# Softmax attention in another order on TensorE, four buffers of turned weights, and changed layer ends

## The chip, the cores and the metric

The kernel runs on one core of a Trainium2 chip. The metric is the device time of one execution in microseconds (us); a smaller number is better. An execution is profiled once, and its time, its span (first to last instruction) and its rows come from that one execution.

## What is computed

The reference runs a transformer of four layers over 512 tokens of width 1024, in float32. The first two layers also carry 256 context tokens. They have a gated linear attention, a neighbourhood attention and a sliding-window attention; the last two have an attention over selected keys and an mLSTM. Each layer ends in a gated feed-forward network (FFN). The part that the change reorders is the softmax of these attentions, cut here to what it comes to:

```python
s_loc = einsum('bnqhgd,bnkhd->bhgnqk', qb, kb) * scale      # local keys, masked with -inf
s_ctx = einsum('bnqhgd,blhd->bhgnql', qb, kc) * scale       # context keys
p = softmax(concatenate([s_loc, s_ctx, s_sink], axis=-1))   # s_sink only in the sliding window
o = einsum('bhgnqk,bnkhd->bnqhgd', p_loc, vb) + einsum('bhgnql,blhd->bnqhgd', p_ctx, vc)
```

## The kernel before, in words

The program is written by hand for each engine: the order of the code is the order in which an engine runs it, and semaphores tie the engines together. There is no scheduler. A layer is: norm and modulation of the activations, the input projection (`product`, L611), the token mixers, the output projection, the FFN (`gate_up` L1082, then `product` again), and a layer end. Products are in float32 made of three matmuls of rounded parts: each operand is split into a high part (L1319 for weights, L1327 for activations, on ACT) and a low part (L1823 and L1835 on DVE).

**The softmax loop.** `softmax_attention` works through units; a unit is one head by one tile of 128 queries against n keys. Two units make a pair p. Layer 0 has 36 pairs: 6 of 256 keys, 12 of 512, 6 of 256, and then 12 of the sliding window (3 of 512, 6 of 640, 3 of 512). Layer 1 has the 24 of these that are not of 256 keys. Layers 2 and 3 have 16 each: 4 of 128, 4 of 256, 4 of 384 and 4 of 512 keys, in that order. For one unit:

- PE computes the scores, queries by keys (`scores`, L825 and L826, both units of a pair together).
- DVE adds the bias or mask, negates, and takes the row extreme (`weigh`, L1908) into one of four score buffers SB.
- ACT takes the exponential in place and the row sum (`exp`, L1489).
- PE transposes the weights in blocks of 128 by 128 (`turned`, L838) into bank PS[4] for the even unit, PS[5] for the odd.
- The turned weights are copied to a buffer PB: the even unit by DVE (L1947), the odd by ACT (L1504). There are two such buffers, one for each.
- PE multiplies the turned weights with the values (`values`, L851) into bank PS[7].
- After each group of units DVE divides by the row sum (`output`, L1924 to L1933), which frees PS[7].

PE's order in a pair is: turn both units, scores of pair p+1, values of both units. DVE's order is: copy of the even unit, weigh the two units of pair p+1. ACT's is: copy of the odd unit, then two exponentials of pair p+1.

**The start of a layer's projection.** `turn_normed` and `turn_norm` transpose the normed activations, one f for each 128 of their 1024 columns (L644 for f = 0 and 1, L632 for the others; six tiles each). ACT and DVE split each into high and low parts. In layer 1 the first chunk of the product goes through f (there called k) in turn, four tiles and 12 matmuls of 428 columns for each; it waits for the low part (`normed_low0`). The transposes of f = 4 to 7 (`turn_beside`) stand between the parts of the product.

**The layer end.** After the last product PE runs `warm(8)` (L571), 16 matmuls on constants whose result nobody reads. In the meantime DVE adds the gated result to the residual and ACT sums its squares (L1447). In layer 1 the mean and root go through eight small ACT operations (L1457, L1458) and four square roots (L1462). In layers 2 and 3 GpSimd (POOL) multiplies the FFN's output with a gain (L1291) while DVE adds it tile by tile to the residual (L2437). DVE's last reciprocal (L2576) ends the layer. Then all engines meet at a barrier (L2659), behind which the next layer's first operations start (L1356 on ACT, L1805 on DVE). There is no barrier inside a layer.

## Time and profile before

| | |
|---|---|
| time, median of 3 runs | 3622.78 us (3615.99 to 3623.82) |
| time of the profiled execution | 3606.66 us |
| its span | 3604.9 us |
| its mean granted TensorE clock | 0.959 of full speed |
| PE busy | 3352.9 us (93% of the span) |
| PEld (weight loads) busy | 2721.4 us (75%) |
| DVE busy | 2003.1 us (56%) |
| ACT busy | 1122.1 us (31%) |
| POOL busy | 194.1 us (5%) |
| 16 DMA engines | 92 GB/s of reads and writes of HBM over the span |

Busy is the time in which an engine runs an instruction; PEld is the loading of a matmul's stationary operand, which overlaps the matmul before. The granted clock is the share of TensorE's full clock that the chip gave it: 1.00 is 2.4 GHz and 0.50 is 1.2 GHz, and an average between them is a mixture in time. A share of the whole span says little about one stage; the stages are read by window.

### The profile page before, as it was taken

To read this page: it belongs to the slowest core of one execution; us is meant where nothing else is said; L and a number is where in the kernel's file an instruction comes from. 1 tells how busy PE (TensorE), PEld (TensorE's weight loads), DVE (VectorE), ACT (ScalarE), POOL (GpSimd) and SP (SyncE) were. 2 spreads that over 40 slices of the span, in tenths; PEclk is the share of its full clock that TensorE was granted. 3 is DMA by queue.
4 is the path that set the end of the run, shared out by engine and by line. 5 is a ranking of instruction groups with operands and counts; after the bars stand their busy time and mean duration, and the time that the engine had idled before them with its cause. 6 is when DMAs were issued, how large, how long until landed. Compare 5 with 4: busy or idle time off the path is not lost. (4 is left out here: it accounts for less than half of the span.)

```text
span 3604.9 us, 44421 instructions
## 1 busy us (share of the span) xinstructions
PE 3352.9 (93%) x17758; PEld 2721.4 (75%) x17758; DVE 2003.1 (56%) x3595; ACT 1122.1 (31%) x1926; POOL 194.1 (5%) x187
## 2 busy tenths in 40 slices
PE   6998999999999997999999998799999998699998
PEld 4986777888888895777877775467877775468886
DVE  4666655846564425557555556667445555653334
ACT  3113454111112412442222433542222433542222
POOL 0000000000000000000000143000000242000001
PEclk9998999999999997999999997799999997899999
DMA  5441102533231211117444230026443230023332
GB/s 207 131 133 39 51 19 74 152 98 113 94 114 58 68 45 42 52 55 227 151 140 135 74 94 30 1 75 212 154 150 115 88 87 18 0 65 100 92 101 76
DMA packets 316574, 336.23 MB, mean 93 GB/s; under 512 B 11944, under 2 KB 219344, under 8 KB 316368
## 3 DMA queue, kind: packets, MB, share of 16 engines
q1 hardware_dynamic: 316368, 333.39, 29.7%
q8 instruction: 141, 2.31, 0.3%
q14 instruction: 65, 0.53, 0.1%
HBM read 329.67 MB, written 3.67 MB: 92 GB/s over the span
## 5 line engine op out<-in xcount | busy, mean ns | idle before, releaser
L1823 DVE TENSOR_TENSOR weights_low<-weights,weights_high 128x1024 fp32r<-128x1024 f32 (+5 forms) x416 | 488.0, 1175 | 850.2 <-ACT weights_high L1319 848.6
L1319 ACT ACTIVATE weights_high<-weights 128x1024 fp32r<-128x1024 f32 (+5 forms) x416 | 419.8, 1011 | 1311.9 <-PE banks L611 874.8
L1082 PE MATMUL banks<-h_high,weights_high 128*128 128x512 f32 (+1 forms) x1760 | 655.5, 372 | 20.7 <-DVE h_low L1835 12.8
L1082 PE MATMUL banks<-h_low,weights_high 128*128 128x512 f32 (+1 forms) x1760 | 648.8, 369 | 0.0
L1082 PE MATMUL banks<-h_high,weights_low 128*128 128x512 f32 (+1 forms) x1760 | 648.4, 368 | 0.0
L611 PE MATMUL banks<-weights_high,h_high 128*128 128x512 f32 (+4 forms) x1360 | 509.3, 374 | 11.4 <-DVE h_low L1835 6.7
L611 PE MATMUL banks<-weights_high,h_low 128*128 128x512 f32 (+4 forms) x1360 | 500.6, 368 | 0.0
L611 PE MATMUL banks<-weights_low,h_high 128*128 128x512 f32 (+4 forms) x1360 | 499.0, 367 | 0.0
L1082 PEld LDWEIGHTS banks<-h_high,weights_high 128*128 128x128 f32 x1760 | 332.1, 189 | 87.8 <-DVE h_low L1835 14.4
L1082 PEld LDWEIGHTS banks<-h_high,weights_low 128*128 128x128 f32 x1760 | 332.0, 189 | 56.0
L1082 PEld LDWEIGHTS banks<-h_low,weights_high 128*128 128x128 f32 x1760 | 332.4, 189 | 52.7
L611 PE MATMUL banks<-weights_high,hidden_high 128*128 128x512 f32 x792 | 311.1, 393 | 15.3 <-DVE weights_low L1823 15.3
L611 PE MATMUL banks<-weights_high,hidden_low 128*128 128x512 f32 x792 | 309.0, 390 | 0.0
L611 PE MATMUL banks<-weights_low,hidden_high 128*128 128x512 f32 x792 | 308.9, 390 | 0.0
L611 PEld LDWEIGHTS banks<-weights_high,h_high 128*128 128x128 f32 x1360 | 257.3, 189 | 54.2 <-issue 21.4
L611 PEld LDWEIGHTS banks<-weights_high,h_low 128*128 128x128 f32 x1360 | 257.1, 189 | 28.5
L611 PEld LDWEIGHTS banks<-weights_low,h_high 128*128 128x128 f32 x1360 | 257.6, 189 | 27.3 <-issue 1.0
L2545 DVE TENSOR_TENSOR projected<-projected,banks 128x512 f32<-128x512 f32 (+1 forms) x110 | 69.7, 634 | 253.3 <-PE banks L1082 240.8
L1735 ACT ACTIVATE projected<-banks 128x512 f32<-128x512 f32 (+1 forms) x110 | 61.1, 556 | 445.9 <-PE banks L1082 445.7
L611 PEld LDWEIGHTS banks<-weights_high,hidden_high 128*128 128x128 f32 x792 | 149.1, 188 | 52.0 <-DVE weights_low L1823 20.4
L851 PEld LDWEIGHTS banks<-projected,scratch 128*128 128x128 f32 x1232 | 155.4, 203 | 43.2 <-issue 38.2
L611 PEld LDWEIGHTS banks<-weights_high,hidden_low 128*128 128x128 f32 x792 | 149.0, 188 | 31.4
(338 smaller groups left out, 4114.2 us busy)
## 6 DMA issues: line engine op xcount, KB each, us to landing
projected<-in_w_mod SPq DMA_DIRECT2D x44, 1024.0 KB, 6.4
weights<-in_w_gate_up SPq DMA_DIRECT2D x88, 512.0 KB, 3.9
weights<-in_w_down SPq DMA_DIRECT2D x80, 512.0 KB, 3.8
extra<-in_w_mod SPq DMA_DIRECT2D x36, 1024.0 KB, 6.3
weights<-in_w_in SPq DMA_DIRECT2D x48, 512.0 KB, 3.7
weights<-in_w_gate SPq DMA_DIRECT2D x44, 512.0 KB, 4.7
weights<-in_w_up SPq DMA_DIRECT2D x44, 512.0 KB, 3.9
weights<-in_w_mod SPq DMA_DIRECT2D x32, 512.0 KB, 3.9
```

The costliest lines, as they stand in the source:

```text
L611: mm = pe.matmul(out_banks[t][:, 0:n], x[:, kk - off[0], at], wt[:, kk - k, :], start=(kk == k0 and q == 0), stop=(kk == k1 - 1 and q == 2))
L851: mm = pe.matmul(out, PB[i % 2][:, j * PT:(j + 1) * PT], v, start=(j == 0), stop=(j == len(u["v"]) - 1))
L1082: mm = pe.matmul(bank[:, 0:cnt], wt[:, k, :], x[:, k, a - GOFF:a - GOFF + cnt], start=(k == 0 and q == 0), stop=(k == KD - 1 and q == 2))
L1319: act.activation(WH[s_ % 2][:, 0:k * n], slots[j % LAND][:, 0:k * n], ACT.Copy).then_inc(S["w_high"], 1)
L1735: act.activation(SG[q % 2][:, 0:cnt], bank[:, 0:cnt], ACT.Silu).then_inc(S["emptied_act"], 1)
L1823: dve.tensor_tensor(WL[s_ % 2][:, 0:k * n], slots[split_of[s_] % LAND][:, 0:k * n], WH[s_ % 2][:, 0:k * n].bitcast(F32), ALU.subtract).the ...
L2545: dve.tensor_tensor(FT[:, 0:cnt], SG[q % 2][:, 0:cnt], bank[:, 0:cnt], ALU.mult)
```

## The change

In the softmax loop PE's order becomes: scores of pair p+1, turn the two units of pair p, values of pair p-1. The loop runs one iteration more. There are four buffers of turned weights; the new two lie in a free part of EX (layers 0 and 1) or of SC (2 and 3). DVE weighs before it copies, and divides a group one pair later; ACT takes the first of the two exponentials before its copy. The other edits: in layer 1 the transposes of f = 2 and 3 move behind the product's parts k = 0 and k = 1 (`turn_between`). The warm-up at a layer end goes from 16 matmuls to 8 (layer 0), 18 (layer 1) and 22 (layer 2). At the end of layer 1 twelve small ACT operations become four DVE operations (`gained_means`) and one square root. GpSimd's eight multiplications in each of layers 2 and 3 go to DVE, behind its read of the product.

```diff
         SB = [SC[:, 8448 + 640 * i:8448 + 640 * (i + 1)] for i in range(4)]
-        PB = [SC[:, 11008 + 640 * i:11008 + 640 * (i + 1)] for i in range(2)]
+        PB = [SC[:, 11008 + 640 * i:11008 + 640 * (i + 1)] for i in range(2)] + [EX[:, 640 * i:640 * (i + 1)] for i in range(2)]
         MASKS = SC[:, 12288:12288 + M_N]
...
         SB = [SC[:, 6144 + 512 * i:6656 + 512 * i] for i in range(4)]
-        PB = [SC[:, 9728 + 512 * i:10240 + 512 * i] for i in range(2)]
+        PB = [SC[:, a:a + 512] for a in (9728, 10240, 10752, 12288)]
         pairs = [(0, 2), (1, 3), (4, 6), (5, 7)]
...
                                 mm.then_inc(B.filled, 1)
+                        if between:
+                            between(first)
                     if kn == k1:
...
                     there[f] = low_done
-                for f in range(ahead, 4):
-                    there[f] = turn_norm(turned0, IN_T, f)
+
+            def turn_between(kk):
+
+                if not start_loads and not second and kk < 2:
+                    there[2 + kk] = turn_norm(turned0, IN_T, 2 + kk)
...
                         lambda i: (turn_beside(4 * j + i), mods_beside(4 * j + i), gates_beside(4 * j + i), index_beside(4 * j + i)), None if j else B,
-                        "emptied_dve" if start_loads else "normed_low0")
+                        "emptied_dve" if start_loads else "normed_low0", None if j else turn_between)
             mods_beside(n_slots)
...
                     for j, v in enumerate(u["v"]):
-                        mm = pe.matmul(out, PB[i % 2][:, j * PT:(j + 1) * PT], v, start=(j == 0), stop=(j == len(u["v"]) - 1))
+                        mm = pe.matmul(out, PB[i % 4][:, j * PT:(j + 1) * PT], v, start=(j == 0), stop=(j == len(u["v"]) - 1))
                     mm.then_inc(S["mix_values"], 1)
...
                     warm(3, 6)
-                for p in range(len(units) // 2):
-                    turned(2 * p)
-                    turned(2 * p + 1)
+                for p in range(len(units) // 2 + 1):
                     if p + 1 < len(units) // 2:
                         scores(p + 1)
-                    values(2 * p)
-                    values(2 * p + 1)
+                    if p < len(units) // 2:
+                        turned(2 * p)
+                        turned(2 * p + 1)
+                    if p:
+                        values(2 * p - 2)
+                        values(2 * p - 1)
                 pe.wait_ge(S["mix_out"], group_of(units, len(units) - 1) + 1)
...
             if following:
-                warm(8)
+                warm(11 if second else 4 if with_ctx else 9)
             assert len(release) == len(weight_units)
...
                 pool.tensor_copy(VA[:, :, :, 0:128], PW[:, :, M_V:M_V + 512].rearrange("p t (h e) -> p t h e", e=128)).then_inc(S["v_ones"], 1)
-                for j in range(2):
-                    half = slice(512 * j, 512 * (j + 1))
-                    for i in range(LAT_T):
-                        pool.wait_ge(S["emptied_dve"], weighed_at[j] + i + 1)
-                        pool.tensor_tensor(YGV[:, i, half], YBV[:, i, half], GBV[:, 1, 0, half], ALU.mult).then_inc(S["y_gained"], 1)
...
                 for i0 in (0, 2):
-                    two = slice(i0, i0 + 2)
                     for i in (i0, i0 + 1):
...
                         last_square(XV[:, OUT_T[i]], 1, i, SQ_RIGHT)
-                    for i in (i0, i0 + 1):
-                        step(act.activation(MEAN_SQ[:, i:i + 1], SQ_RIGHT[:, i:i + 1], ACT.Identity, scale=1.0 / D, bias=SQ_BIAS[:, i:i + 1]))
-                        step(act.activation(SQ2_BIAS[:, i:i + 1], MEAN_SQ[:, i:i + 1], ACT.Identity, scale=EPS, bias=SQ2_LEFT[:, i:i + 1]))
+                    if i0:
+                        act.sem_inc(S["first_squared"], 1)
                     for i in (i0, i0 + 1):
...
                         last_square(XGV[:, i], 1, i, SQ2_RIGHT)
-                        act.activation(R_X[:, i:i + 1], SQ2_RIGHT[:, i:i + 1], ACT.Sqrt, scale=1.0 / D,
-                                       bias=SQ2_BIAS[:, i:i + 1]).then_inc(S["end_root"], 1)
+                act.sem_inc(S["second_squared"], 1)
+                act.wait_ge(S["second_mean"], 1)
+                act.activation(R_X[:, 0:LAT_T], SQ2_RIGHT, ACT.Sqrt).then_inc(S["end_root"], LAT_T)
...
                     nb = min(u["n"], 512)
+                    if 2 * p + 3 < len(units):
+                        exp(2 * p + 2)
                     act.wait_ge(S["mix_turn"], 2 * p + 2)
-                    if p:
-                        act.wait_ge(S["mix_values"], 2 * p)
-                    act.activation(PB[1][:, 0:nb], PS[5][:, 0:nb], ACT.Copy).then_inc(S["mix_turned_act"], 1)
+                    if p >= 2:
+                        act.wait_ge(S["mix_values"], 2 * p - 2)
+                    act.activation(PB[(2 * p + 1) % 4][:, 0:nb], PS[5][:, 0:nb], ACT.Copy).then_inc(S["mix_turned_act"], 1)
                     if u["n"] > 512:
                         for e in range(2):
-                            ins = act.activation(PB[e][:, 512:640], PS[6][:, 128 * e:128 * e + 128], ACT.Copy)
+                            ins = act.activation(PB[(2 * p + e) % 4][:, 512:640], PS[6][:, 128 * e:128 * e + 128], ACT.Copy)
                         ins.then_inc(S["mix_fifth"], 1)
                     if 2 * p + 3 < len(units):
-                        exp(2 * p + 2)
                         exp(2 * p + 3)
...
                 for p in range(len(units) // 2):
-                    if p and first_of_group(units, 2 * p):
+                    if p > 1 and first_of_group(units, 2 * p - 2):
                         output(done)
-                        done = 2 * p
-                    nb = min(units[2 * p]["n"], 512)
-                    dve.wait_ge(S["mix_turn"], 2 * p + 1)
-                    if p:
-                        dve.wait_ge(S["mix_values"], 2 * p - 1)
-                    dve.tensor_copy(PB[0][:, 0:nb], PS[4][:, 0:nb]).then_inc(S["mix_turned_dve"], 1)
+                        done = 2 * p - 2
                     if 2 * p + 3 < len(units):
...
                         weigh(2 * p + 3)
+                    nb = min(units[2 * p]["n"], 512)
+                    dve.wait_ge(S["mix_turn"], 2 * p + 1)
+                    if p >= 2:
+                        dve.wait_ge(S["mix_values"], 2 * p - 3)
+                    dve.tensor_copy(PB[2 * p % 4][:, 0:nb], PS[4][:, 0:nb]).then_inc(S["mix_turned_dve"], 1)
                 output(done)
...
                         copy_out(bank[:, :], y)
+                    if last:
+                        dve.wait_ge(S["emptied_dve"], B.emptied_by("d"))
+                        step(dve.tensor_tensor(YGV[:, t - CTX_T, 512 * half:512 * (half + 1)], y, GBV[:, 1, 0, 512 * half:512 * (half + 1)], ALU.mult))
                     if last and half and t > OUT_T[0]:
...
             halves, lasts = [0], [0]
+
+            def gained_means():
+
+                dve.wait_ge(S["first_squared"], 1)
+                step(dve.scalar_tensor_tensor(MEAN_SQ, SQ_RIGHT[:, 0:LAT_T], 1.0 / D, SQ_BIAS[:, 0:LAT_T], ALU.mult, ALU.add))
+                step(dve.tensor_scalar(SQ2_BIAS, MEAN_SQ, EPS, None, ALU.mult))
+                step(dve.scalar_tensor_tensor(SQ2_BIAS, SQ2_LEFT, 1.0 / D, SQ2_BIAS, ALU.mult, ALU.add))
+                dve.wait_ge(S["second_squared"], 1)
+                dve.scalar_tensor_tensor(SQ2_RIGHT, SQ2_RIGHT, 1.0 / D, SQ2_BIAS, ALU.mult, ALU.add).then_inc(S["second_mean"], 1)
...
```

The lines move by a few numbers: L838 becomes L842, L825 and L826 become L829 and L830, L851 becomes L855, L571 becomes L570, L611, L632 and L644 become L610, L633 and L645, L1908 becomes L1906 and L1947 becomes L1948.

PE at the start of the softmax of layer 0, pairs of 256 keys, before. `scratch` holds the queries, keys, scores and turned weights, `projected` the values, and `constants` holds the identity for a transpose.

```order
L838 MATMUL banks<-constants,scratch 128x128 x4
L825 MATMUL banks<-scratch 128x256
L826 MATMUL banks<-scratch 128x256
L851 MATMUL banks<-projected,scratch 128x64 x4
L838 MATMUL banks<-constants,scratch 128x128 x4
```

The same place in the changed kernel; `extra` is one of the new buffers:

```order
L829 MATMUL banks<-scratch 128x256
L830 MATMUL banks<-scratch 128x256
L842 MATMUL banks<-constants,scratch 128x128 x4
L829 MATMUL banks<-scratch 128x256
L830 MATMUL banks<-scratch 128x256
L842 MATMUL banks<-constants,scratch 128x128 x4
L855 MATMUL banks<-projected,scratch 128x64 x4
L829 MATMUL banks<-scratch 128x256
L830 MATMUL banks<-scratch 128x256
L842 MATMUL banks<-constants,scratch 128x128 x4
L855 MATMUL banks<-projected,extra 128x64 x4
```

Between a pair's transposes (x4) and its values (x4) there stood only the scores of the next pair. Now there stand the scores of the pair after it and that pair's transposes.

DVE in the same stage, one pair, before:

```order
L1947 COPY scratch<-banks 128x256 [waits mix_values,mix_turn]
L1908 ISA scratch,small<-banks,weights 128x256 [waits mix_turn,mix_scores,landed0]
L1908 ISA small 128x1
L1908 ISA scratch,small<-banks,weights 128x256 [waits mix_turn,mix_scores,landed0]
L1908 ISA small 128x1
L1947 COPY scratch<-banks 128x256 [waits mix_values,mix_turn]
```

and in the changed kernel:

```order
L1906 ISA scratch,small<-banks,weights 128x256 [waits mix_turn,mix_scores,landed0]
L1906 ISA small 128x1
L1906 ISA scratch,small<-banks,weights 128x256 [waits mix_turn,mix_scores,landed0]
L1906 ISA small 128x1
L1948 COPY scratch<-banks 128x256 [waits mix_values,mix_turn]
L1906 ISA scratch,small<-banks,weights 128x512 [waits mix_turn,mix_scores,landed0]
```

The copy of a pair's turned weights stood ahead of the weighing of the next pair, and now stands behind it.

PE at the start of layer 1 (f = 1 of the first transposes, f = 2 and 3, then the product), before:

```order
L644 MATMUL banks<-constants,projected 128x128 [waits normed0]
L644 MATMUL banks<-constants,projected 128x128
L632 MATMUL banks<-constants,projected 128x128 [waits normed_low0]
L632 MATMUL banks<-constants,projected 128x128
L632 MATMUL banks<-constants,projected 128x128 [waits normed_low0]
L632 MATMUL banks<-constants,projected 128x128 x3
L632 MATMUL banks<-constants,projected 128x128 [waits normed_low0]
L632 MATMUL banks<-constants,projected 128x128
L632 MATMUL banks<-constants,projected 128x128 [waits normed_low0]
L632 MATMUL banks<-constants,projected 128x128 x3
L611 MATMUL banks<-weights_high,h_high_49 128x428 [waits normed_low0,w_low]
L611 MATMUL banks<-weights_low,h_high_49 128x428
```

The changed kernel, from the last matmul of the product's part k = 0, which follows straight on f = 1:

```order
L610 MATMUL banks<-weights_low,h_high_49 128x428
L610 MATMUL banks<-weights_high,h_low_50 128x428
L633 MATMUL banks<-constants,projected 128x128 [waits normed_low0]
L633 MATMUL banks<-constants,projected 128x128
L633 MATMUL banks<-constants,projected 128x128 [waits normed_low0]
L633 MATMUL banks<-constants,projected 128x128 x3
L610 MATMUL banks<-weights_high,h_high_49 128x428 [waits normed_low0]
L610 MATMUL banks<-weights_low,h_high_49 128x428
L610 MATMUL banks<-weights_high,h_low_50 128x428
```

The six transposes of f = 2 stood ahead of the product and now stand between its parts k = 0 and k = 1; those of f = 3 follow in the same way behind k = 1, straight ahead of those of f = 4.

## Rows read from the trace of the kernel before

**Rows 1.** Windows over the four softmax stages: PE, PEld, DVE, ACT, POOL busy, clock.
```profile
377.00:515.50 138.50, 132.79 (x993) 103.65 (x991) 81.85 (x314) 73.25 (x196) 0.00 (x0) 1.00 0.08 24
1456.80:1560.80 104.00, 102.16 (x797) 83.27 (x795) 60.74 (x208) 54.91 (x134) 0.00 (x0) 1.00 0.10 32
2222.20:2280.30 58.10, 56.29 (x301) 39.91 (x299) 26.48 (x115) 26.88 (x78) 0.00 (x0) 0.77 0.01 1
3021.50:3082.10 60.60, 58.88 (x301) 41.81 (x299) 26.48 (x115) 26.89 (x78) 0.00 (x0) 0.72 0.00 1
```

**Rows 2.** Timeline of PEld, a pair of 512 keys, layer 0: start, duration, [idle before].
```profile
428.69 0.42 PEld L838 LDWEIGHTS banks<-constants,scratch 128*128 128x128 f32 x4 [0.29 <-ACT scratch L1489]
...
432.87 0.42 PEld L838 LDWEIGHTS banks<-constants,scratch 128*128 128x128 f32 x4 [0.29 <-ACT scratch L1489]
```

**Rows 3.** Timeline of PEld, a pair of 256 keys, layer 0.
```profile
385.24 0.20 PEld L838 LDWEIGHTS banks<-constants,scratch 128*128 128x128 f32 x2 [0.37 <-ACT scratch L1489]
```

**Rows 4.** Windows: two pairs of 128 keys (layer 2), two of 256 (layer 0).
```profile
2223.92:2228.05 4.13, 3.34 (x20) 2.20 (x20) 1.60 (x10) 2.31 (x11) 0.00 (x0) 1.00 0.00 0
379.59:385.24 5.65, 5.09 (x32) 3.34 (x32) 2.74 (x16) 2.95 (x11) 0.00 (x0) 1.00 0.01 1
```

**Rows 5.** Timeline of PEld, a pair of 128 keys, layer 2.
```profile
2225.99 0.14 PEld L838 LDWEIGHTS banks<-constants,scratch 128*128 128x128 f32 x1 [0.48 <-ACT scratch L1489]
2226.37 0.14 PEld L838 LDWEIGHTS banks<-constants,scratch 128*128 128x128 f32 x1 [0.24 <-ACT scratch L1489]
```

**Rows 6.** Window: three pairs of 256 keys, layer 2.
```profile
2231.24:2242.87 11.63, 11.63 (x48) 8.48 (x49) 4.55 (x20) 4.74 (x17) 0.00 (x0) 0.50 0.00 0
```

**Rows 7.** Timeline of ACT, layer 2: copies of the odd units of 384 and 512 keys.
```profile
2258.42 0.49 ACT L1504 ACTIVATE scratch<-banks 128x384 f32<-128x384 f32 x1 [0.64 <-PE banks L838]
2261.82 0.49 ACT L1504 ACTIVATE scratch<-banks 128x384 f32<-128x384 f32 x1 [0.64 <-PE banks L838]
...
2274.03 0.60 ACT L1504 ACTIVATE scratch<-banks 128x512 f32<-128x512 f32 x1 [0.74 <-PE banks L838]
2278.10 0.60 ACT L1504 ACTIVATE scratch<-banks 128x512 f32<-128x512 f32 x1 [0.75 <-PE banks L838]
```

**Rows 8.** Timeline at the end of layer 0.
```profile
1174.31 7.03 PE L571 MATMUL banks<-constants 128*128 128x512 f32 x16
...
1177.63 0.19 DVE L2576 RECIPROCAL small<-small 128x6 f32<-128x6 f32 x1 [1.18 <-ACT small L1437]
...
1182.51 2.19 ACT L1356 ACTIVATE projected<-x_res,small 128x1024 f32<-128x1024 f32 x2 [4.98 <-PEq L2659]
```

**Rows 9.** Timeline at the start of layer 1.
```profile
1188.47 1.03 DVE L1835 TENSOR_TENSOR h_low<-projected,h_high 128x512 fp32r<-128x512 f32 x2
...
1191.62 0.70 PE L611 MATMUL banks<-weights_high,h_high 128*128 128x428 f32 x1
...
1195.17 0.69 DVE L1835 TENSOR_TENSOR h_low<-projected,h_high 128x512 fp32r<-128x512 f32 x1 [0.61 <-ACT projected L1333]
...
1197.43 1.47 PE L632 MATMUL banks<-constants,projected 128*128 128x128 f32 x12
...
1198.66 0.44 PE L611 MATMUL banks<-weights_high,h_high 128*128 128x428 f32 x1
```

**Rows 10.** Timeline at the end of layer 1.
```profile
2002.68 7.03 PE L571 MATMUL banks<-constants 128*128 128x512 f32 x16
...
2011.21 0.18 DVE L2576 RECIPROCAL small<-small 128x4 f32<-128x4 f32 x1 [4.04 <-ACT small L1462]
```

**Rows 11.** Timeline at the end of layer 2.
```profile
2800.84 2.26 DVE L2437 SCALAR_TENSOR_TENSOR x_res<-scratch,small,x_res 128x1024 f32<-128x1024 f32 x1
...
2802.48 7.03 PE L571 MATMUL banks<-constants 128*128 128x512 f32 x16
...
2809.26 1.28 DVE L2437 SCALAR_TENSOR_TENSOR x_res<-scratch,small,x_res 128x1024 f32<-128x1024 f32 x1
...
2812.24 0.18 DVE L2576 RECIPROCAL small<-small 128x4 f32<-128x4 f32 x1 [0.42 <-ACT small L1473]
```

More of the change, by code:

```diff
@@ L592, in part_used, with product @@
                 release.append(("unit_part", mine["part"]))
-            def product(ah, al, tt, off, n, k0, k1, by, ready=None, B=B, after=None, behind=None, low="emptied_dve"):
+            def product(ah, al, tt, off, n, k0, k1, by, ready=None, B=B, after=None, behind=None, low="emptied_dve", between=None):
                 out_banks = {}
@@ L1439, in last_squares @@
                 if not j:
-                    if gained is not None:
-                        act.activation(SQ2_LEFT, SQ2_LEFT, ACT.Copy, scale=1.0 / D)
                     left_mean()
```

5 lines of the change are left out of this document (2 added, 3 removed).

## The prediction

> **What bounds the kernel now.** I read the shares first: PE is busy for 93% of the span, but that is a mean over stages, so the next view is the windows over the four softmax stages, where the change works [rows 1]. Together they last 138.5 + 104.0 + 58.1 + 60.6 = 361 us, a tenth of the span. PE shows as busy for all but 5.7, 1.8, 1.8 and 1.7 us of them. That would say that nothing is to be had but for two things. A busy row of PE runs to the modelled end of a matmul, so it hides a part of each stall; the weight loads (PEld) show where PE's queue stood. And the last column but two is the granted clock: 1.00 in layers 0 and 1, 0.77 and 0.72 in layers 2 and 3.
>
> The weight loads show the stall that the present order makes. In a pair of 512 keys the transposes of the second unit start 0.29 us late, behind ACT's exponential (L1489), and the period of a pair is 432.87 - 428.69 = 4.18 us [rows 2]. In a pair of 256 keys the first unit's transposes also wait, 0.37 us [rows 3], the second's another 0.29 as in [rows 2]; the period is 5.65/2 = 2.83 us [rows 4]. In a pair of 128 keys the waits are 0.48 and 0.24 us [rows 5] of a period of 4.13/2 = 2.07 us [rows 4]. So PE waits on the circle scores, weigh, exp, turn of the next pair, with only the values of one pair as cover. Pairs of 640 keys show no such wait.
>
> The clock is a second effect. In layers 2 and 3 it is 1.00 in the first pairs of 128 keys [rows 4] and 0.50 some microseconds later, where three pairs of 256 keys take 11.63 us, or 3.88 each, and PE is busy without a gap [rows 6]. The same pair takes 2.83 in layer 0 at 1.00 [rows 4]. What the engine did ahead of the fall: it went through pairs of 128 keys with 0.72 us of waits for ACT in 2.07 [rows 5]. In layer 0, where the clock stayed, the waits were 0.66 in 2.83 at most [rows 2, 3].
>
> **Part 1, the softmax order.** PE gets the values of pair p-1 and the scores of p+1 as cover around the turn of p: the exponentials of pair p+1 now have a whole period to be done in. The waits of [rows 2, 3, 5] should go. What they give back lies between two bounds: the time in which PE isn't busy at all, and the wait of the loads. For 256 keys that is 0.28 us a pair ((5.65 - 5.09)/2 in [rows 4]) to 0.66 (0.37 + 0.29); I take 0.53, period 2.30, nearer to the upper end as the loads are the queue itself. For 128 keys it is 0.40 to 0.72. Here ACT is next: it is busy 2.31 us in two pairs [rows 4], 1.16 a pair, and three instructions with the gap ahead of each make about 1.45; I take 1.47, a saving of 0.60. For 512 keys 0.10 ((5.7 - 12 x 0.28)/24, the rest of layer 0's idle time over its other pairs) to 0.29; I take 0.15 in layers 0 and 1. Pairs of 384 keys lie between those of 256 and 512: 0.25. In layers 2 and 3 the pairs of 512 keys already run at 4.07 [rows 7]; there 0.10. For 640 keys nothing. The later copies and the later division on DVE cost nothing: DVE is busy 81.85 of 138.5 us [rows 1], and the buffers' wait is now on values of two pairs back; if that cover were gone, a copy (0.49 to 0.60 us [rows 7]) a pair would show. Nothing else is queued on the three engines in this stage. So:
> - layer 0: 12 x 0.53 + 18 x 0.15 = 9.1 us (5.7 to 13)
> - layer 1: 18 x 0.15 = 2.7 us (1.8 to 5.2)
> - layers 2 and 3, each: 4 x (0.60 + 0.53 + 0.25 + 0.10) = 5.9 us (1.8 to 8)
>
> **Part 2, the clock in layers 2 and 3.** At full clock the 16 pairs of before would take 4 x (2.07 + 2.83 + 3.40 + 4.07) = 49.5 us, with 3.40 from the two copies of 384 keys and 4.07 from those of 512 [rows 7]. The stages took 58.1 and 60.6 us [rows 1], so the lower clock cost at most 8.6 and 11.1 us; I take 8 and 10.5, since the windows have edges. If it holds at 1.00 now, that comes back. What speaks for it: the clock fell behind the stretch with the longest waits in a pair, and there the order takes most of them away; the same work in layer 0, with shorter ones, kept 1.00 for 138.5 us. Between the bounds, 0 and 19.7 for both layers, I take a value near the upper, because the new stretch will be nearer to layer 0's than to its own of before. It is the least certain step.
>
> In this trace, bursts of matmuls with small gaps between them keep 1.00 over the 138.5 and 104.0 us of layers 0 and 1 and lose it in layers 2 and 3 [rows 1]. The Trainium skill, "TensorE: Matmul & The Clock Gate", section "A second HAM failure mode: psum-queue depth-cycling", describes a matmul kernel in which small idle times between groups of matmuls made the clock swing to and fro. By that rule the gaps that ACT leaves in pairs of 128 keys are enough to lose the clock again, and part 2 would be 0; by the row of layer 0, which has such gaps and holds, it is 18.5 us. The rule is rival 1.
>
> **Part 3, the layer ends.**
> - Layer 0: PE's 16 warm matmuls run 1174.31 to 1181.34, DVE's last reciprocal ends at 1177.82, and the barrier opens behind PE, at about 1181.4, with ACT's first at 1182.51 [rows 8]. Eight matmuls end at 1174.31 + 3.5 = 1177.8, level with DVE. Saving 3.4 us (bounds 3.0 and 3.5). The price without the warming, a lower clock at the next start, is in part 4's range.
> - Layer 1: PE ends at 2009.71, DVE at 2011.39 [rows 10]. Twelve small ACT operations with DVE's wait of 4.04 us on them go, for which DVE gets four; I estimate its end 1.8 us earlier. But 18 matmuls instead of 16 end at 2009.71 + 0.87 = 2010.58, so PE is late next. Saving 0.8 us (0.5 to 1.8).
> - Layer 2: DVE ends at 2812.42, PE's 22 matmuls would end at 2802.48 + 7.03 + 6 x 0.43 = 2812.1 [rows 11]. DVE's additions (L2437) take 2.26 us while GpSimd multiplies beside them and 1.28 alone [rows 11], so they lose 1.0 each, and DVE gains 0.69 for each multiplication of half a tile (the price that this L1835 has for 128x512 [rows 9]). Near the end, one against two: about even. Saving 0.3 us (-1 to 1.5), and the same in layer 3, which has no warm-up.
>
> **Part 4, the start of layer 1.** The first product starts at 1191.62 and needs only f = 0 low, done at about 1189.0 (half of L1835's row at 1188.47); the transposes of f = 2 and 3 stood between. It can now start 2.6 us earlier, but nothing behind it is bound by that. Part k = 2 needs f = 2 and the transposes of f = 4 and 5, and those wait for the low part of f = 3. Before, f = 3 was low at 1195.86, PE was through with k = 1 at 1197.43, did the 12 transposes and began k = 2 at 1198.66 [rows 9]. The parts k = 0 and k = 1 took 5.8 us together. Now k = 0 runs from 1189.0, and as an estimate takes 4.3 us, since more of it falls into the time of the lower clock, then f = 2 takes 1.1 and k = 1 2.4, and f = 3 is transposed at about 1197.5; the splits by ACT and DVE take some 3 us more, to 1200.6, and k = 2 begins at about 1201.3. That is 2.6 us later (bounds: 1 earlier, if the clock and the splits are quick, and 3.5 later).
>
> **The sum.** 9.1 + 2.7 + 2 x 5.9 + 18.5 + 3.4 + 0.8 + 0.6 - 2.6 = 44.3 us. The profiled execution took 3606.66 us (span 3604.9 and 1.8 around it), so its like would take 3562. It was 16 us under the median of the runs, 3622.78; on the median the forecast is 3578.5 us.
>
> **Rivals.**
> 1. The order helps, but the clock falls again in layers 2 and 3. At half clock PE is busy without a gap [rows 6], so the order gives almost nothing in those pairs: 4 x 0.60 us in the pairs of 128 keys, some 2.5 us a layer, are left of 5.9 and the clock's 9. Gain 9.1 + 2.7 + 5 + 2.2 = 19, median 3604. For it: the last pairs ahead of the fall are the shortest, and ACT leaves gaps in them. Chance 0.20. That it falls in one of the two layers alone (about 3591): 0.13.
> 2. The change doesn't do what it says: PE is the bound already, as its busy rows have it, and the waits of the loads only move elsewhere (to L851 or L825). Then only PE's own idle time of 11 us could come back, and half of it is likely; with the clock as before, 3 to 9 us, median about 3617. Against it: the wait of L838 on ACT is one of the queue, not of an overlap. Chance 0.05.
> 3. Slower: the new interleaving loses the clock in layers 0 and 1, where it holds now. A pair of 256 keys costs 3.88 us at half clock against my 2.30, so 1.6 us a pair, and longer pairs more. All 60 pairs would cost 95 us, median about 3670; it decides from 44.3/1.6 = 28 pairs on. Against it: nothing in these stages gets less dense. Chance 0.02.
>
> The forecast itself has 0.60. Its own range is 3563 to 3588, from the bounds of parts 1, 3 and 4 and a few microseconds between medians. The whole range is 3560 to 3606, which takes in rival 1. Faster or slower counts from 0.2%, 7 us, which is about what separates the runs of before: faster 0.94 (the forecast, rival 1 and part of rival 2), same 0.04, slower 0.02.
>
> **What would show it.** The granted clock of the two late softmax stages at 1.00 and their length near 44 us; periods between ACT's copies of 1.5, 2.3, 3.15 and 4.0 us for 128, 256, 384 and 512 keys; no wait of L842 on the exponential; in layer 0 a stage 9 us shorter; PE's warming at the end of layer 0 level with DVE's last reciprocal; part k = 2 in layer 1 beginning some 20 us after the barrier's release instead of 17. The prediction is wrong if the clock falls in the pairs of 128 keys though their waits are shorter, if ACT's copy turns out late and PE waits at L855 in place of L842, or if layer 0's stage loses its 1.00.

## The result, and the profile after

The changed kernel takes 3563.28 us (median of 4 runs, 3561.32 to 3565.77) against 3619.39 us of the kernel before (3612.22 to 3623.82). The ratio is 0.9842, 95% interval [0.9822, 0.9862]: 56 us less. The profiled execution took 3561.32 us with a span of 3559.5 us, 45.4 us under the span of before. The forecast was 3578.5 us, range 3560 to 3606; the chance on faster was 0.94. So the direction is as forecast and the time lies inside the range, 3 us above its lower end; the gain is a quarter larger than the 44 us of the sum.

The windows over the changed kernel's stages come first. The first four reach from the last work ahead of a softmax stage to the first matmul of the output projection (in layers 2 and 3 with the mLSTM in them); then the softmax of layers 2 and 3 alone, and two pairs of 128 keys. Columns as in [rows 1].

```profile
373.74:511.60 137.86, 133.62 (x1054) 111.86 (x1055) 90.89 (x340) 76.52 (x216) 0.00 (x0) 1.00 0.10 32
1445.05:1556.02 110.97, 106.95 (x848) 90.76 (x847) 67.63 (x224) 56.46 (x144) 0.00 (x0) 0.98 0.11 34
2201.55:2337.99 136.44, 104.24 (x562) 70.70 (x563) 92.15 (x224) 68.40 (x163) 4.01 (x2) 0.86 0.01 2
2985.59:3122.94 137.35, 104.80 (x564) 70.97 (x563) 92.37 (x225) 68.41 (x163) 4.02 (x2) 0.86 0.01 3
2211.50:2251.50 40.00, 39.19 (x291) 30.55 (x292) 25.23 (x115) 25.68 (x78) 0.00 (x0) 1.00 0.01 2
2996.00:3036.00 40.00, 39.18 (x291) 30.54 (x292) 25.23 (x115) 25.68 (x78) 0.00 (x0) 1.00 0.01 2
2213.61:2216.75 3.14, 3.07 (x25) 2.30 (x24) 1.69 (x10) 2.18 (x11) 0.00 (x0) 1.00 0.01 3
```

The same four stretches of the kernel before:

```profile
369.29:522.19 152.90, 144.20 (x1055) 111.00 (x1055) 93.48 (x340) 80.87 (x216) 0.00 (x0) 1.00 0.09 29
1449.18:1564.39 115.21, 111.23 (x847) 89.30 (x847) 68.36 (x223) 59.20 (x144) 0.00 (x0) 1.00 0.11 32
2212.62:2366.32 153.70, 120.62 (x562) 79.45 (x563) 93.36 (x224) 70.17 (x163) 4.01 (x2) 0.78 0.01 2
3012.31:3168.30 155.99, 123.00 (x563) 81.14 (x563) 93.36 (x224) 70.18 (x163) 4.02 (x2) 0.77 0.01 2
```

The differences are 15.0, 4.2, 17.3 and 18.6 us, 55.2 in all. That is as much as the whole gain of the medians. The clock of the two late softmax stages is 1.00 where it was 0.77 and 0.72 [rows 1]. The busy time of the weight loads hardly moved where the clock had been full (111.9 against 111.0 us in layer 0): the same work stands closer together.

PEld's timeline of a pair of 512 keys in layer 0 of the changed kernel:

```profile
425.11 0.86 PEld L842 LDWEIGHTS banks<-constants,scratch 128*128 128x128 f32 x8 [0.33 <-issue]
425.94 1.86 PEld L855 LDWEIGHTS banks<-projected,extra 128*128 128x128 f32 x16
427.87 0.18 PEld L829 LDWEIGHTS banks<-scratch 64*128 64x128 f32 x1
...
428.93 0.86 PEld L842 LDWEIGHTS banks<-constants,scratch 128*128 128x128 f32 x8 [0.33 <-issue]
```

The period is 428.93 - 425.11 = 3.82 us, against 4.18 [rows 2]. The wait for ACT is gone, and the eight loads of both units run in one row. One short pause is left, where the scores go over into the transposes. The kernel before had, beside the wait of 0.29 us [rows 2], two more in each pair, ahead of the scores and ahead of the values:

```profile
429.28 0.18 PEld L825 LDWEIGHTS banks<-scratch 64*128 64x128 f32 x1 [0.17 <-issue]
...
430.34 1.86 PEld L851 LDWEIGHTS banks<-projected,scratch 128*128 128x128 f32 x16 [0.33 <-issue]
```

So 0.79 us of pauses became 0.33 and a gap of 0.07 ahead of the scores. And a pair of 128 keys in layer 2:

```profile
2214.17 0.53 PEld L855 LDWEIGHTS banks<-projected,scratch 128*128 128x128 f32 x4
...
2215.40 0.29 PEld L842 LDWEIGHTS banks<-constants,scratch 128*128 128x128 f32 x2 [0.33 <-issue]
2215.57 0.57 PEld L855 LDWEIGHTS banks<-projected,scratch 128*128 128x128 f32 x4
...
2216.35 0.18 PEld L829 LDWEIGHTS banks<-scratch 64*128 64x128 f32 x1 [0.21 <-DVE small L1906]
```

Here 0.54 us of pauses are left. ACT is not the engine that limits these pairs: it is busy 2.18 of the 3.14 us of the last window above, and it waits for DVE's weighing:

```profile
2215.99 0.51 ACT L1486 ACTIVATE scratch<-scratch,small 128x256 f32<-128x256 f32 x1 [0.49 <-DVE small L1906]
```

Some pauses of the loads ahead of the transposes (L842) are still put down to ACT's exponential, 0.33 us at 2216.98 and in pairs of 256 keys. They are no longer than the one of 0.33 us above that is put down to nothing (`issue`), and PE itself runs on through them.

The layer ends, as in [rows 8], [rows 10] and [rows 11]; first layer 0, then 1, then 2:

```profile
1168.18 3.59 PE L570 MATMUL banks<-constants 128*128 128x512 f32 x8
...
1171.51 0.19 DVE L2587 RECIPROCAL small<-small 128x6 f32<-128x6 f32 x1 [1.18 <-ACT small L1437]
...
1172.94 2.19 ACT L1356 ACTIVATE projected<-x_res,small 128x1024 f32<-128x1024 f32 x2 [1.54 <-PEq L2670]
...
1994.41 7.89 PE L570 MATMUL banks<-constants 128*128 128x512 f32 x18
...
2001.23 0.18 DVE L2587 RECIPROCAL small<-small 128x4 f32<-128x4 f32 x1 [0.33 <-ACT small L1460]
...
2003.50 1.15 ACT L1356 ACTIVATE projected<-scratch,small 128x1024 f32<-128x1024 f32 x1 [2.31 <-PEq L2670]
...
2774.58 9.60 PE L570 MATMUL banks<-constants 128*128 128x512 f32 x22
...
2783.99 0.18 DVE L2587 RECIPROCAL small<-small 128x4 f32<-128x4 f32 x1 [0.50 <-ACT small L1470]
```

In layer 0 PE ends at 1171.77, DVE at 1171.70: level. In layer 1 PE ends at 2002.30, 0.9 us behind DVE's 2001.41, so the barrier waits for it. In layer 2 both end at 2784.2.

The start of layer 1, as in [rows 9]:

```profile
1189.86 0.44 PE L633 MATMUL banks<-constants,projected 128*128 128x128 f32 x2 [0.58 <-DVE h_low L1833]
1191.47 0.66 PE L633 MATMUL banks<-constants,projected 128*128 128x128 f32 x4 [1.17 <-DVE h_low L1833]
1191.88 0.44 PE L610 MATMUL banks<-weights_high,h_high 128*128 128x428 f32 x1
...
1199.41 0.44 PE L610 MATMUL banks<-weights_high,h_high 128*128 128x428 f32 x1
```

Part k = 2 begins at 1191.88, 18.9 us behind the barrier's release (1172.94), where it was 16.15 [rows 8, 9]. The transposes ahead of it wait 0.58 and 1.17 us for the low part of f = 3. The long block of products behind f = 7 begins at 1199.41, 26.5 us behind the release. From part k = 2 to that block (24 matmuls and the 12 transposes of f = 6 and 7) the changed kernel takes 7.53 us and the kernel before 6.00. PE is busy throughout in both; what differs is the clock. The changed kernel, a part of the same stretch, and the kernel before:

```profile
1191.88:1199.41 7.53, 7.53 (x39) 7.13 (x38) 3.99 (x8) 4.13 (x7) 0.00 (x0) 0.77 0.21 58
1192.60:1195.80 3.20, 3.20 (x10) 2.98 (x9) 2.52 (x6) 2.39 (x4) 0.00 (x0) 0.50 0.49 136
```

```profile
1198.66:1204.66 6.00, 6.00 (x39) 5.77 (x38) 4.37 (x8) 4.51 (x8) 0.00 (x0) 1.00 0.26 73
```

Behind the waits of 0.58 and 1.17 us the clock fell to 0.50 for over 3 us.

### The profile page after: what moved, and what is told of

Its sections match the earlier page's. It is cut to its first block and busy times, and to the rows that moved or that the text cites. A ratio compares the mean times of both kernels' runs of the same rounds, so it can differ in the third digit from the quotient of the medians.

```text
span 3559.5 us, 44419 instructions
## 1 busy us (share of the span) xinstructions
PE 3311.6 (93%) x17758; PEld 2712.8 (76%) x17758; DVE 2003.3 (56%) x3615; ACT 1108.3 (31%) x1914; POOL 173.8 (5%) x171
## 3 DMA queue, kind: packets, MB, share of 16 engines
q8 instruction: 141, 2.31, 0.3%
## 5 line engine op out<-in xcount | busy, mean ns | idle before, releaser
L610 PE MATMUL banks<-weights_high,h_high 128*128 128x512 f32 (+4 forms) x1360 | 510.1, 375 | 13.9 <-DVE h_low L1833 9.0
L610 PE MATMUL banks<-weights_high,h_low 128*128 128x512 f32 (+4 forms) x1360 | 501.3, 369 | 0.0
L610 PE MATMUL banks<-weights_low,h_high 128*128 128x512 f32 (+4 forms) x1360 | 499.5, 367 | 0.0
L610 PE MATMUL banks<-weights_high,hidden_high 128*128 128x512 f32 x792 | 311.9, 394 | 16.0 <-DVE weights_low L1821 16.0
L610 PE MATMUL banks<-weights_low,hidden_high 128*128 128x512 f32 x792 | 309.7, 391 | 0.0
L610 PE MATMUL banks<-weights_high,hidden_low 128*128 128x512 f32 x792 | 309.5, 391 | 0.0
L610 PEld LDWEIGHTS banks<-weights_high,h_high 128*128 128x128 f32 x1360 | 257.7, 190 | 57.4 <-issue 24.2
L610 PEld LDWEIGHTS banks<-weights_high,h_low 128*128 128x128 f32 x1360 | 257.2, 189 | 28.6
L610 PEld LDWEIGHTS banks<-weights_low,h_high 128*128 128x128 f32 x1360 | 258.0, 190 | 27.3 <-issue 1.0
L610 PEld LDWEIGHTS banks<-weights_high,hidden_high 128*128 128x128 f32 x792 | 149.4, 189 | 52.8 <-DVE weights_low L1821 21.0
L610 PEld LDWEIGHTS banks<-weights_high,hidden_low 128*128 128x128 f32 x792 | 149.4, 189 | 31.6
L610 PEld LDWEIGHTS banks<-weights_low,hidden_high 128*128 128x128 f32 x792 | 149.5, 189 | 30.6
```

What stands on the lines that cost most here:

```text
L610: mm = pe.matmul(out_banks[t][:, 0:n], x[:, kk - off[0], at], wt[:, kk - k, :], start=(kk == k0 and q == 0), stop=(kk == k1 - 1 and q == 2))
```

## The experiments

All ratios are to the kernel before, with a 95% interval; e1 to e4, e5 to e8 and e9 to e11 ran as three groups, each on one chip.

**e1, the kernel before again.** No edit.

> The kernel before once more, unchanged, for a second profile of it. In the two profiles so far the change gains 45.4 us, but the medians differ by 56 us, and the profiled execution of before was 6 to 17 us quicker than its timed ones. Theory A (the rest is the granted clock in stages that the change does not touch, which differs from execution to execution): this profile shows a span nearer to 3615 us, and the difference to the first profile lies in stages with a lower granted clock. In the two late softmax stages the clock falls again, at 55 to 58 us from the first copy to the last. Theory B (the kernel before has a stage that differs in length at the same clock, a transfer for example): the difference lies in a stage at clock 1.00. Ratio to before: 1.000.

Measured: 3623.35 us, ratio 1.0009 [0.9997, 1.002]; span 3620.3 us. Theory A holds. The span is 15.4 us longer than in the first profile. Of this, 3.9 us lie ahead of the first softmax stage, 4.0 between the output projection and the end of layer 0 (mostly FFN) and 6.7 between the end of layer 0 and the softmax of layer 1. The first two windows of e1:

```profile
251.00:381.00 130.00, 101.10 (x859) 78.17 (x859) 83.32 (x173) 38.34 (x63) 0.00 (x0) 0.79 0.16 51
600.00:660.00 60.00, 52.92 (x295) 44.82 (x296) 41.49 (x67) 23.37 (x37) 0.00 (x0) 0.89 0.41 119
```

and of the first profile of the kernel before:

```profile
251.00:377.00 126.00, 98.12 (x857) 75.20 (x857) 83.00 (x173) 38.44 (x63) 0.00 (x0) 0.82 0.16 53
600.00:660.00 60.00, 55.40 (x331) 47.30 (x330) 45.20 (x71) 20.88 (x33) 0.00 (x0) 0.97 0.47 139
```

The same stage of the FFN gets 0.89 in one execution and 0.97 in the other. The late softmax stages are the same in both profiles to 0.1 us, the fall of the clock with them. So the first profile of before was a lucky one by some 15 us, and 56 us, not 45, is the gain.

**e2, the order alone.** The kernel before with the edits to the softmax loop and to PB only:

```diff
+                for p in range(len(units) // 2 + 1):
                     if p + 1 < len(units) // 2:
                         scores(p + 1)
+                    if p < len(units) // 2:
+                        turned(2 * p)
+                        turned(2 * p + 1)
+                    if p:
+                        values(2 * p - 2)
+                        values(2 * p - 1)
```

> Before with the new softmax order and the four buffers alone; layer ends and the start of layer 1 as before. Theory A (the terms add up by stage): the softmax stages give some 55 us as in the changed kernel (15 in layer 0, 5 in layer 1, 17 and 19 in layers 2 and 3), since all the other edits together came to -0.7 us in the trace (ends -3.4, -0.8, -0.3, starts +4.3, -2.0, +1.5). Time within 4 us of the changed kernel's 3563, ratio 0.984 to 0.986. Theory B (the layer ends carry a good part of the gain, because less warming changes the clock of what follows): 10 us or more above it, ratio 0.987 or more.

Measured: 3562.72 us, ratio 0.9851 [0.9827, 0.9874], span 3561.3 us. Theory A holds: the order is the gain, and the rest cancels. Counted from the last warm matmul ahead of layer 1's softmax to the output projection, both profiles of the kernel before take 108.0 us, this one and the changed kernel 101.4.

**e3, all but the order.** The changed kernel with the softmax loop of before.

> The changed kernel with the softmax loop of before: layer ends, transposes between the product's parts and the multiplications on DVE as changed. Theory A: no change to speak of, -0.7 us by the sum of the traces, ratio 0.998 to 1.001, and the clock falls in layers 2 and 3's softmax as before. Theory B: 10 us faster or more, ratio under 0.997.

Measured: 3613.91 us, ratio 0.9992 [0.9977, 1.0006]. Theory A holds by the ratio, though the median lies 8 us under that of the kernel before on this chip; the runs of either spread over 15 us and more. The two late stages took 58.1 and 58.0 us from the first copy to the last: the clock fell again. In layer 2 that is 2.6 us more than in the kernel before, with the same loop.

**e4, without the transposes in between.** The changed kernel, and:

```diff
+                for f in range(ahead, 4):
+                    there[f] = turn_norm(turned0, IN_T, f)
-            def turn_between(kk):
...
-                        "emptied_dve" if start_loads else "normed_low0", None if j else turn_between)
+                        "emptied_dve" if start_loads else "normed_low0")
```

> The changed kernel with the transposes of f = 2 and 3 back ahead of the first product of layer 1. Theory A (they are late there, and f = 3's split holds up f = 5 and part k = 2): from the barrier's release to the long block of the product's chunk in layer 1 it takes 22.2 us instead of 26.5, so 4.3 us less, time about 3559. Rival (the clock alone made that stage longer, since the product starts at half clock whatever stands ahead of it): no difference beyond 1 us, and the stage keeps its 26 us.

Measured: 3555.97 us (3 under the 3559 expected), ratio 0.9827 [0.9804, 0.985], span 3548.8 us. Layer 1's release and the start of its long block, in its timeline:

```profile
1167.05 2.19 ACT L1351 ACTIVATE projected<-x_res,small 128x1024 f32<-128x1024 f32 x2 [1.53 <-PEq L2665]
...
1189.14 0.44 PE L610 MATMUL banks<-weights_high,h_high 128*128 128x428 f32 x1
```

That is 1189.14 - 1167.05 = 22.1 us, as theory A had it, against 26.5. The edit costs the changed kernel 4.4 us: 2.8 because part k = 2 begins later, and 1.5 because the clock falls behind the waits, which it doesn't here (6.00 us from k = 2 to the long block). So the rival has a part in it. The other 6 us between the two spans lie in stages that are the same code (the clock again).

**e5, two buffers.** The changed kernel with `PB[i % 2]`, and the copies' waits one pair tighter:

```diff
-                    if p >= 2:
-                        dve.wait_ge(S["mix_values"], 2 * p - 3)
-                    dve.tensor_copy(PB[2 * p % 4][:, 0:nb], PS[4][:, 0:nb]).then_inc(S["mix_turned_dve"], 1)
+                    if p:
+                        dve.wait_ge(S["mix_values"], 2 * p - 1)
+                    dve.tensor_copy(PB[0][:, 0:nb], PS[4][:, 0:nb]).then_inc(S["mix_turned_dve"], 1)
```

> The changed kernel with two buffers of turned weights in place of four: the copies then wait for the values of the pair before (p-1), which PE runs behind the transposes of pair p. Theory A (the order carries the gain, the buffers little): a copy takes 0.28 to 0.69 us, and PE's scores of the next pair, 0.6 to 0.9 us, stand between the values and the transposes that need the bank back, so they cover it. The four softmax stages lengthen by 0 to 5 us in all, the clock holds, ratio to before 0.984 to 0.987. Rival (the buffers are what lets the order work): PE waits for a copy in each of the 92 pairs, some 0.4 us, 35 us in all, and the clock may fall again; ratio 0.993 or more.

Measured: 3569.64 us, ratio 0.986 [0.9842, 0.9878]. The four stretches take 143.3, 113.8, 139.3 and 140.4 us, 14.3 us more than in the changed kernel, of which some 6 show in its median. The clock held at 1.00 in both late stages. The ratio is the one expected; the size in the stretches was missed, though the rival is further off. The copies now wait for values, 0.43 and 0.33 us in pairs of 128 keys in layer 2:

```profile
2217.99 0.29 DVE L1948 COPY scratch<-banks 128x128 f32<-128x128 f32 x1 [0.43 <-PE banks L855]
...
2218.20 0.28 ACT L1503 ACTIVATE scratch<-banks 128x128 f32<-128x128 f32 x1 [0.33 <-PE banks L855]
```

Long pairs cover it (512 keys: 3.84 us in place of 3.82), others don't (256 keys: 2.30 for 2.06 to 2.26; 640 keys, with a fifth block to copy: 4.84 for 4.70). By the traces' stretches the order gives some 41 us of the 55 with two buffers, and the buffers give the other 14; the medians would leave the buffers some 6.

**e6, one wait of before filled.** The kernel before, and:

```diff
                 for p in range(len(units) // 2):
+                    if second and 0 < p < 4:
+                        warm(1, 6)
                     turned(2 * p)
                     turned(2 * p + 1)
```

> The kernel before with one more warm matmul of 512 columns (result not used) ahead of the transposes of the second, third and fourth pair of 128 keys in layers 2 and 3, where PE waits 0.48 us for ACT. It takes 0.43 us at full clock. Theory A (PE's waits in these pairs are what the clock fell behind): the clock holds, the two stages take 48 us from the first copy to the last in place of 55.5 and 58, the time falls by 16 to 18 us, ratio 0.995. Rival (something else makes it fall, such as the kind of work or what stands ahead of the stage): the stages stay at 55 to 58 us and the ratio at 0.999 to 1.001; then the new order held the clock by more than by filling that one wait.

Measured: 3604.19 us, ratio 0.9952 [0.9936, 0.9969]. Theory A holds. Windows over the two late softmax stages:

```profile
2244.10:2294.20 50.10, 47.85 (x307) 32.44 (x305) 26.49 (x115) 26.92 (x78) 0.00 (x0) 1.00 0.01 1
3035.80:3085.80 50.00, 47.81 (x307) 32.44 (x305) 26.48 (x115) 26.88 (x78) 0.00 (x0) 1.00 0.00 1
```

The call makes two matmuls, not the one of the expectation, so six in each stage with no use; a pair of 128 keys takes 2.14 us in place of 2.07. They hold the clock at 1.00 and take 8.3 and 10.3 us off the two stretches (153.70 to 145.44 us and 155.99 to 145.73).

**e7, the ends.** As e4, with 16 warm matmuls at the end of layer 1:

```diff
-                warm(11 if second else 4 if with_ctx else 9)
+                warm(11 if second else 4 if with_ctx else 8)
```

> The changed kernel with the transposes of f = 2 and 3 back ahead of the product (as in the kernel without them in between) and 16 instead of 18 warm matmuls at the end of layer 1, where PE's last one ended 0.9 us behind DVE. Theory A: the stretch from DVE's reciprocal to the next layer's first operation goes from 2.1 to 1.2 us; time 1 us under the kernel without transposes in between (3556), not to be told from it by the medians. Rival: less warming ahead of the barrier lowers the clock at the start of layer 2 and gives back 1.5 us there.

Measured: 3554.4 us, ratio 0.9816 [0.9797, 0.9834]. From DVE's reciprocal to the next layer's first operation it takes 1.2 us in place of 2.1, as theory A had it. But the next layer's softmax begins 204.4 us behind the first product instead of 202.7, since that product starts at a clock of 0.50 instead of 1.00. So the rival is right too, and the trace shows no net gain.

**e8, warm matmuls at the starts.** As e7, and:

```diff
+                warm(1, 0)
                 for f, low_done in enumerate(turn_normed(0, turned0, IN_T, normed0_by, range(ahead))):
                     there[f] = low_done
+                warm(2 if second else 1, 0)
```

In the trace a call with 1 is two matmuls, and one with 2 is four.

> As the one before it, and with warm matmuls (result not used) at the starts of layers 1 to 3: one ahead of the first transposes, and one (layer 1) or two (layers 2 and 3) behind those of the first f, where PE waits for the low parts. Theory A (the half clock at a layer's start comes from PE's pauses at and behind the barrier): the first product runs at full clock sooner, 1 to 2 us less in each of the three starts, time about 3551. Rival: the warm matmuls themselves run at half clock, 0.9 us each, and push transposes back: 1 to 2 us more in each.

Measured: 3551.83 us, ratio 0.9805 [0.9786, 0.9825]. Theory A holds in the trace: from the release to the softmax stage the three layers take 2.2, 1.0 and 2.9 us less than in e7. The medians differ by 2.6 us, and the intervals overlap; e11 is the better proof.

**e9, a pause put back.** The changed kernel, and:

```diff
                     if p < len(units) // 2:
+                        if second and p < 4:
+                            pe.wait_ge(S["mix_exp"], 2 * p + 3)
                         turned(2 * p)
```

> The changed kernel with a pause put back: in the first four pairs of layers 2 and 3 (128 keys) PE waits, ahead of the transposes of pair p, for the first exponential of pair p+1, some 0.8 to 1.0 us in each. Filling such a wait in the kernel before held the clock. Theory A (PE's pauses in these pairs are what the clock falls behind): it falls in both layers again; the pairs of 256 keys take about 3.8 us in place of 2.1, and the two stages lengthen by 3 to 4 us for the pauses and 8 to 12 for the clock, 25 us in all, ratio 0.990 to 0.992. Rival (the new order holds the clock in another way, since scores, transposes and values now follow each other without a break): the stages lengthen by the pauses alone, 7 us in all, ratio 0.986.

Measured: 3578.88 us, ratio 0.9889 [0.9863, 0.9915]. The clock fell in both layers. PE's transposes of two pairs of 128 keys, and windows over the stretch of low clock and the one behind it in layers 2 and 3:

```profile
2213.55 0.45 PE L842 MATMUL banks<-constants,scratch 128*128 128x128 f32 x2 [0.93 <-ACT scratch L1488]
2215.35 0.44 PE L842 MATMUL banks<-constants,scratch 128*128 128x128 f32 x2 [0.93 <-ACT scratch L1488]
```

```profile
2217.50:2227.80 10.30, 9.10 (x38) 6.73 (x38) 4.79 (x26) 3.92 (x15) 0.00 (x0) 0.50 0.01 2
2226.00:2260.00 34.00, 34.00 (x252) 27.07 (x250) 20.19 (x81) 20.68 (x53) 0.00 (x0) 0.97 0.01 1
3006.00:3019.70 13.70, 11.11 (x47) 8.33 (x47) 5.54 (x33) 5.35 (x21) 0.00 (x0) 0.50 0.01 2
3019.00:3051.00 32.00, 32.00 (x241) 25.79 (x240) 19.64 (x80) 19.64 (x53) 0.00 (x0) 0.99 0.00 1
```

The stretches take 6.7 and 9.0 us more than in the changed kernel, 15.7 in place of the 25 expected (the medians of this run and e10, on the same chip, differ by 15.2): with the new order the clock is back after 10.3 and 13.7 us, where before it stayed at 0.50 through the pairs of 256 keys [rows 6], 27 and 34 us in all. By my estimate the pauses alone are some 2.8 us of each stretch (4 x 0.7); that leaves 3.9 and 6.2 us to the clock. So neither theory has the size: the fall is that of theory A, the length lies between the two.

**e10, the changed kernel again.** No edit.

> The changed kernel once more, beside the next one on the same chip. Median 3563 within 3 us, ratio 0.984. In its profile the softmax stages measure as in the first (137.9, 111.0, 136.4 and 137.4 us from the last transposes ahead of the stage to the output projection) within 1 us, apart from layer 1, where the clock at the start differs by up to 3.

Measured: 3563.66 us, ratio 0.9843 [0.9825, 0.9861]. The four stretches are 137.9, 111.4, 136.5 and 137.3 us, as expected. At the start of layer 1 parts k = 2 and k = 3 take 6.3 us again (4.8 in the kernel before): the low clock there is in both profiles.

**e11, the kernel of e8 again.**

> The version without transposes in between, with 16 warm matmuls at the end of layer 1 and warm matmuls at the starts, once more and beside the changed kernel. By the traces it gains 4.3 + 0.9 + 2 + 1 + 3 = 11 us on the changed kernel: median about 3552, ratio to before 0.981. If the gain were a matter of the chip of that run, it would be within 4 us of the changed kernel.

Measured: 3549.24 us, ratio 0.9803 [0.9787, 0.9819], 14 us under the changed kernel on the same chip, 11 being expected; the intervals of e10 and e11 don't meet. Windows of e11 over the starts of layers 1 and 3, and of e10 over that of layer 3:

```profile
1173.31:1193.90 20.59, 17.60 (x101) 14.70 (x101) 15.97 (x26) 16.68 (x25) 0.00 (x0) 1.00 0.24 65
2778.48:2792.80 14.32, 13.74 (x87) 11.91 (x87) 10.61 (x15) 10.00 (x14) 0.00 (x0) 1.00 0.51 148
```

```profile
2783.16:2800.30 17.14, 14.27 (x81) 13.94 (x81) 10.61 (x15) 9.96 (x14) 0.00 (x0) 0.80 0.44 124
```

The start of layer 3 takes 14.3 us at a clock of 1.00 in place of 17.1 at 0.80, to the same point of the product.

## Why the prediction was right, point by point

- **Part 1, the order: the mechanism is right (e2, e3), the size too small.** Layers 0 and 1 gave 15.0 and 4.2 us for 9.1 and 2.7. In layers 2 and 3 e6 has the clock held with the old order, 145.44 and 145.73 us; the changed kernel has 136.44 and 137.35, so the order gave 9.0 and 8.4 us for 5.9 each. In layer 1 the head of the stretch ran at a lower clock (0.98 over the whole); e2, where it did not, gave 6.3 us. The term that was too small is that of the pairs of 384 and 512 keys. For 512 keys the upper bound was the wait for ACT, 0.29 us, and I took 0.15; the period went from 4.18 to 3.82, 0.36 less, above the bound. The wait went, and with it the pause of 0.17 us between the transposes and the scores; the one of 0.33 us behind the scores stayed. A bound taken from one wait leaves out the small pauses that the reordering removes with it. Pairs of 640 keys, for which nothing was put, went from 4.80 to 4.70 us. In layers 2 and 3 the pairs of 512 keys had 0.10 us each and ran at 3.4 to 3.8 in place of 4.07.
- The prices of short pairs were right: from one copy on ACT to the next it takes 1.46 us for 128 keys in layer 2 (1.47 foreseen) and 2.31 for 256 keys (2.30); 384 keys take 3.02 (3.15). But for 128 keys the reason isn't borne out, so the 1.47 is in part luck: it was three ACT instructions end to end, and ACT waits 0.47, 0.49 and 0.33 us for DVE's weighing in the last three. The late stages' length, given as near 44 us, is under 40: the windows of 40.00 us above hold them whole.
- The copies' cover: part 1 priced the buffers at nothing while values two pairs back release them. With two buffers (e5) it would have been 14 us. The later division on DVE, also put at nothing, shows in one wait of PE in each softmax stage but layer 1's, 0.16 us in layer 0 and 0.4 in layers 2 and 3.
- **Part 2, the clock: right in sign, size and place.** 8 and 10.5 us were foreseen, and e6 measures 8.3 and 10.3 with no change of order. It was the least certain step, and e6 and e9 show its cause from both sides: filling one wait of 0.48 us in three pairs holds the clock, and putting waits of 0.93 us back drops it. Rival 1 didn't happen. One reading was off: the waits of layer 0 were not 0.66 us in a pair at most. At 394.63, where the pairs of 512 keys begin, the loads waited 0.85 and then 0.29 us for ACT, and the clock stayed at 1.00; so one longer wait by itself didn't drop it there. By the Trainium skill, "TensorE: Matmul & The Clock Gate", section "A second HAM failure mode: psum-queue depth-cycling", small pauses between groups of matmuls swing the clock. e9 agrees in that the clock goes from 1.00 to 0.50 behind the pauses and back. The pauses left in the changed kernel (0.54 us in a pair of 128 keys) didn't do it.
- **Part 3, the ends: right.** Release against the start of the warming: layer 0 4.76 us for 8.20, 3.4 less as foreseen. Layer 1: 9.09 for 9.9, 0.8 less, with PE the late one, as foreseen. Layer 2: both engines level, 0.3 less, as foreseen. Layer 3: from the last matmul's end to the end of the span 11.8 us for 12.2, 0.4 less for 0.3 foreseen.
- What part 3 left out: the clock at the next start. Layer 2's start took 2.0 us less and layer 3's 1.5 more than before, at 0.50 for more or less of the first product. By the traces of e8 and e11 this is worth 6 us over three starts.
- **Part 4, the start of layer 1: right in sign, and the sum stopped too early.** Part k = 2 came 2.8 us later, for 2.6 foreseen. But the waits ahead of it had a price of their own, which the sum didn't have: the clock fell to 0.50 behind them, and the same matmuls and transposes took 7.53 us in place of 6.00. With these 1.5 us the long block is 4.3 us later, over the bound of 3.5, and e4, without the waits, gives it back. Part 4 had put the lower clock into k = 0 alone.
- **The sum against the median.** The profile of before was 15 us quicker than that of e1 in stages without an edit, so 44.3 us forecast stand against 56 on the medians; 55.2 lie in the softmax stretches. The ends and starts, 2.2 us of gain in the sum, cancel to within about 1 us in the traces, as e2 says by its median.
- Rival 2 (PE's busy rows are the bound, 3 to 9 us) is refuted by e2: PE's busy time itself went from 144.2 to 133.7 us in layer 0, since a busy row of PE holds a part of the stall. Rival 3 (slower, the clock falls in layers 0 and 1) isn't seen: 1.00 in layer 0, 0.98 in layer 1.

What stays open: which pause exactly the clock falls behind in layers 2 and 3 and at the start of layer 1, and why the same code gets 0.89 or 0.97 in the FFN of layer 0. No run here varies these alone.

## What to carry to other kernels

Where two matmul stages with a softmax between them alternate on TensorE, put a whole further group's work between the stage that needs ACT and the one that feeds it, and give the copies as many buffers as the order is deep: here, by the traces, the order was worth 41 us and the buffers 14. Price a reordering by the idle time of the weight loads over a whole period, not by the one wait that it aims at. Before anything is reordered for a low clock, fill one pause with useless matmuls: one line, in three pairs of a layer, showed here what 19 us of half clock hung on. And where a reordering leaves new waits, look at the clock behind them: at the start of layer 1 it cost 1.5 us on top of the 2.8 of the later start.

## What was not expected of the hardware

The effect of the granted clock was repeatable to 0.1 us in some places (the late softmax stages of the kernel before, in two profiles, though the same loop in e3 took 2.6 us more in layer 2) and went by chance in others. Layer 0, from the output projection to the warming at its end, took 652.1 us in one profile of the kernel before and 656.1 in the other, and the start of layer 1, from the release to the first copy of turned weights, 275.4 or 282.1 us in the same code. A difference of 15 us between the spans of two single profiles of this kernel can come wholly from stages that nobody edited; look at the stage of the edit.
